# W1's blocks as the stationary operand, with 256 tokens moving, in a two-layer decoder trunk

## The chip, the cores and the metric

The kernel runs on one core of a Trainium2 chip. Its engines work side by side and meet only at semaphores: TensorE (PE, with its weight loads as PEld), VectorE (DVE), ScalarE (ACT), GpSimd (POOL), and SyncE (SP), which here issues most DMAs. The metric is the time of one execution on the device in microseconds; lower is better.

## The reference

Sequence 256, width 2048, two layers, everything in float32. Each layer has a mixer (layer 0 causal pooling, layer 1 retention) and then an MLP of hidden width 8192 with a squared ReLU. Before every sub-layer x is normalized, scaled and shifted.

```python
def sq_relu_mlp(h, w1, w2):
    a = jax.nn.relu(h @ w1)
    return (a * a) @ w2

for i in range(DEPTH):
    mod = jnp.einsum('bd,sdk->bsk', cond, ada_w[i]) + ada_b[i]
    ...
    h = modulate(rmsnorm(x, norm_g[i, 0]), shift_t, scale_t)
    ...                       # pool_mixer or retention
    x = x + gate_t[:, None, :] * y
    h = modulate(rmsnorm(x, norm_g[i, 1]), shift_m, scale_m)
    x = x + gate_m[:, None, :] * sq_relu_mlp(h, mlp_w1[i], mlp_w2[i])
return rmsnorm(x, final_g)
```

## The kernel before

**Matmuls in three products.** Every float32 operand is split into an upper part in the type fp32r and the rest, also in fp32r: `w_hi` and `w_lo` for weights, `h_hi` and `h_lo` for the normalized input (kept transposed: features on the partitions, 16 blocks of 128, by 256 tokens), `a_hi` and `a_lo` for the input of the second matmul. A product is low*high + high*low + high*high, added up in PSUM. On the tensor engine one operand is loaded as a block of 128x128 (the stationary one), the other is moved through it column by column.

**Chunks and units.** Weights come in chunks of 256 rows by 512 columns (512 KB are counted each) through a ring of four: SP loads `raw`, ACT writes `w_hi` (L970), DVE writes `w_lo` (L1343), PE uses both and reports with `w_used`. A chunk is 2 blocks of 128 rows x 2 tiles of 128 tokens x 3 products = 12 matmuls (L555): the tokens' block is stationary, and 512 columns of weights move. The result has tokens on the partitions and 512 outputs along the row, one PSUM bank for each of the two token tiles (`acc[pair][t]`). Eight chunks are a unit: 512 outputs over all of the 2048 inputs. A half unit has four.

**The MLP.** `mlp` goes through groups of eight units. Units 0 to 3 take W1 and make 4 x 512 hidden values, units 4 to 7 take W2 with them. ACT evacuates a W1 unit with ReLU into `ev[u % 2]` and squares it there. W2 needs the squares with the hidden index on the partitions, so in unit u + 1, behind chunk 2, PE transposes the squares (`transpose_squares`, L654): eight transposes of 128x128 in two banks `tb`; ACT copies each bank into `a_hi` (`evacuate_T`, L991), DVE makes `a_lo` from the bank and `a_hi` (`lower_T`, L1585). Seven W1 units are cut in two: their first halves (`p1`, PARTS) run ahead of everything, while the modulation weights are still loading, and are kept in `part_tile`; later `half_unit` does the rest and DVE adds the kept part (`add_part`, L1458). The first unit of layer 1's MLP has a form of its own, `first_unit`, since its input arrives tile by tile.

**Order.** Each engine has its own program, written out by hand from the same loops: `steps` on ACT and DVE puts one weight chunk's part at each step, four chunks ahead of PE, and `hooks` puts other work behind a step. Modulation weights (`ada_w`) are loaded and summed on DVE between chunks, as many as `ADA_SPREAD` and `ADA_EVEN` say. `Count` keeps for each engine how often each semaphore has counted at that place; `TB` counts banks of transposes or what takes their place, `TL` splits into `a_lo`.

## Time and profile before

| | |
|---|---|
| time, median of 3 runs | 2417.39 us (2416.83 to 2421.26) |
| the profiled execution | 2414.45 us |
| its span, first to last instruction | 2412.6 us |
| mean granted TensorE clock | 0.985 |
| busy: PE / PEld / DVE / ACT / POOL | 2339.1 / 1857.2 / 1580.9 / 1086.6 / 22.2 us |
| DMA | 620.38 MB, mean 257 GB/s |

The span is shorter than the execution's time by what lies around the first and last instruction. The busy time of PE is from the starts and the modelled ends of matmuls that overlap each other; the distance from one start to the next is what a matmul costs. Durations in the rows are of this one execution.

### The profile page before, as it was taken

The page shows a single profiled execution, that of the slowest core. Times are in us where ns is not written, and L with a number is a line of the kernel's source. Part 1 is how long each engine was busy: PE and PEld are TensorE (multiplying, and loading weights), DVE is VectorE, ACT ScalarE, POOL GpSimd, SP SyncE. Part 2 cuts the span into 40 slices and gives each one's busy share as a digit, 9 for nine tenths or more (in the row PEclk, how much of TensorE's full clock was granted, in tenths as well). Part 3 has the DMA queues.
Part 4 walks back from the last instruction along what each step waited for, and adds up shares of the span by engine and source line. Part 5 has one row for each costly group of instructions (what it writes and reads, how often), then busy time and mean ns, then how long its engine had stood idle before and what let it go on. Part 6 is the DMA issues. An engine that isn't in the chain of part 4 may idle for free.

```text
span 2412.6 us, 30003 instructions
## 1 busy us (share of the span) xinstructions
PE 2339.1 (97%) x10397; PEld 1857.2 (77%) x10397; DVE 1580.9 (66%) x1654; ACT 1086.6 (45%) x1352; POOL 22.2 (1%) x32
## 2 busy tenths in 40 slices
PE   6689999999999999999999999999999999999998
PEld 2147788887888887888888888887888888888886
DVE  4579886776776887656566657566876445445455
ACT  2324554443443545444444444445543443443443
POOL 0000000000000000000000000000000000000000
PEclk8799999999999999999999999999999999999999
DMA  9999988887887986776666766766987666656654
GB/s 391 405 408 391 343 312 310 296 291 253 296 291 258 327 309 213 239 224 222 220 222 228 240 221 216 228 221 198 331 292 229 185 191 193 185 190 192 188 182 154
DMA packets 269156, 620.38 MB, mean 257 GB/s; under 512 B 19064, under 2 KB 19400, under 8 KB 268112
## 3 DMA queue, kind: packets, MB, share of 16 engines
q1 hardware_dynamic: 267520, 612.44, 74.9%
q0 software_dynamic: 880, 5.77, 0.7%
q8 instruction: 90, 1.47, 0.2%
q14 instruction: 58, 0.48, 0.1%
q10 hardware_dynamic: 608, 0.22, 0.0%
HBM read 616.26 MB, written 2.10 MB: 256 GB/s over the span
## 4 chain that ended last, share of the span: by engine, by line
PE 89%; DMA 5%; DVE 4%; issue 1%; ACT 1%; SPq 0%; ACTq 0%; POOLq 0%; POOL 0%; DVEq 0%
PE acc L555 83%; DMA ada_early_h<-in_ada_w 3%; PE tb L654 2%; DMA raw<-in_mlp_w 1%; DVE ada_acc L1349 1%; DVE w_lo L1343 1%; PE mod_ps L690 0%; DMA ada_raw<-in_ada_w 0%; PE score_ps L904 0%; PE score_ps L690 0%; DVE h_lo L1537 0%; SPq L407 0%; ACT w_hi L970 0%; PE mod_ps L662 0%; PE acc L914 0%
## 5 line engine op out<-in xcount | busy, mean ns | idle before, releaser
L1343 DVE TENSOR_TENSOR w_lo<-raw,w_hi 128x1024 fp32r<-128x1024 f32 x776 | 947.1, 1224 | 725.4 <-ACT w_hi L970 725.0
L970 ACT ACTIVATE w_hi<-raw 128x1024 fp32r<-128x1024 f32 x776 | 821.7, 1060 | 1147.7 <-PE acc L555 1077.8
L555 PE MATMUL acc<-w_hi,h_lo 128*128 128x512 f32 x1792 | 706.9, 394 | 13.2 <-issue 7.0
L555 PE MATMUL acc<-w_hi,h_hi 128*128 128x512 f32 x1792 | 698.9, 390 | 0.0
L555 PE MATMUL acc<-w_lo,h_hi 128*128 128x512 f32 x1792 | 698.4, 390 | 0.0
L555 PE MATMUL acc<-w_hi,a_lo 128*128 128x512 f32 x1312 | 516.4, 394 | 0.0
L555 PE MATMUL acc<-w_hi,a_hi 128*128 128x512 f32 x1312 | 511.1, 390 | 0.0
L555 PE MATMUL acc<-w_lo,a_hi 128*128 128x512 f32 x1312 | 510.8, 389 | 0.0
L555 PEld LDWEIGHTS acc<-w_hi,h_lo 128*128 128x128 f32 x1792 | 337.2, 188 | 89.0 <-issue 12.3
L555 PEld LDWEIGHTS acc<-w_hi,h_hi 128*128 128x128 f32 x1792 | 337.0, 188 | 70.7
L555 PEld LDWEIGHTS acc<-w_lo,h_hi 128*128 128x128 f32 x1792 | 337.4, 188 | 69.5 <-issue 1.4
L1349 DVE SCALAR_TENSOR_TENSOR ada_acc<-ada_raw,cond,ada_acc 128x1024 f32<-128x1024 f32 x240 | 306.9, 1279 | 10.7 <-DMA ada_raw<-in_ada_w 10.4
L555 PEld LDWEIGHTS acc<-w_hi,a_lo 128*128 128x128 f32 x1312 | 246.5, 188 | 60.5 <-issue 8.5
L555 PEld LDWEIGHTS acc<-w_lo,a_hi 128*128 128x128 f32 x1312 | 246.6, 188 | 52.2 <-issue 1.9
L555 PEld LDWEIGHTS acc<-w_hi,a_hi 128*128 128x128 f32 x1312 | 246.4, 188 | 51.7
L986 ACT ACTIVATE ev<-acc 128x512 f32<-128x512 f32 x121 | 64.6, 584 | 7.7 <-PE acc L555 6.4
L1349 DVE SCALAR_TENSOR_TENSOR ada_acc<-ada_early_h,cond,ada_acc 128x1024 f32<-128x1024 f32 x37 | 47.5, 1283 | 26.1 <-DMA ada_early_h<-in_ada_w 25.6
L1585 DVE TENSOR_TENSOR a_lo<-tb,a_hi 128x512 fp32r<-128x512 f32 x80 | 51.3, 682 | 0.0
L690 PE MATMUL mod_ps<-ada_early_h,cond 128*32 128x512 f32 x88 | 29.3, 762 | 19.1 <-DMA ada_early_h<-in_ada_w 19.1
L991 ACT ACTIVATE a_hi<-tb 128x512 fp32r<-128x512 f32 x80 | 42.7, 586 | 0.0
L1001 ACT ACTIVATE sq_junk<-x 128x512 bf16<-128x512 f32 x46 | 28.4, 619 | 29.6 <-DVE x L1498 16.8
L1230 ACT ACTIVATE ev<-ev 128x512 f32<-128x512 f32 x64 | 36.7, 627 | 0.0
(164 smaller groups left out, 756.0 us busy)
## 6 DMA issues: line engine op xcount, KB each, us to landing
raw<-in_mlp_w SPq DMA_DIRECT2D x512, 512.0 KB, 4.5
ada_raw<-in_ada_w SPq DMA_DIRECT2D x280, 512.0 KB, 6.0
raw<-in_ret_w_in SPq DMA_DIRECT2D x192, 512.0 KB, 3.9
ada_early_h<-in_ada_w SPq DMA_DIRECT2D x84, 512.0 KB, 13.1
raw<-in_ret_w_out SPq DMA_DIRECT2D x64, 512.0 KB, 4.2
ada_early_a<-in_ada_w SPq DMA_DIRECT2D x20, 512.0 KB, 10.0
raw<-in_pool_w SPq DMA_DIRECT2D x8, 512.0 KB, 12.6
x<-in_x SPq DMA_DIRECT2D x2, 1024.0 KB, 9.8
```

Source lines behind the costliest of these rows:

```text
L555: mm = nc.tensor.matmul(acc[pair][t][:], l[:, CK * c + j, tok], w[:, c % RING, j, :], start=first and j == 0 and i == 0, stop=last and j = ...
L654: tr = nc.tensor.transpose(tb[b][:, j * S + t * P:j * S + (t + 1) * P], source(t)[:, m * P:(m + 1) * P], ident[:])
L690: mm = nc.tensor.matmul(bank[32 * b:32 * b + 32, :], cond[:, k:k + 1].to_broadcast([P, 32]), raw_rows[:, b % 2 * NB:(b % 2 + 1) * NB], sta ...
L970: nc.scalar.activation(w_hi[:, o % RING], raw[:, o % RING], ACT.Copy).then_inc(hi_ready, 1)
L986: nc.scalar.activation(target[:, t, :], acc[pair][t][:], func).then_inc(evac, 1)
L991: nc.scalar.activation(targets, tb[b][:].rearrange("p (k t) -> p k t", k=2), ACT.Copy).then_inc(tevac, 1)
L1001: nc.scalar.activation(sq_junk[:, t, :], x[:, t, block_ * NB:(block_ + 1) * NB], ACT.Square, accum_out=ssq[:, t, block_:block_ + 1]).then_ ...
L1230: nc.scalar.activation(ev[:, u % 2, t, :], ev[:, u % 2, t, :], ACT.Square).then_inc(sq_done, 1)
L1343: nc.vector.tensor_tensor(w_lo[:, o % RING], raw[:, o % RING], w_hi[:, o % RING].bitcast(F32), ALU.subtract).then_inc(lo_ready, 1)
L1349: nc.vector.scalar_tensor_tensor(out=part, in0=raw_rows, scalar=cond[:, k:k + 1], in1=part, op0=ALU.mult, op1=ALU.add).then_inc(ada_done, 1)
L1585: nc.vector.tensor_tensor(a_lo[:, k:k + 2, :], tb[b][:].rearrange("p (k t) -> p k t", k=2), a_hi[:, k:k + 2, :].bitcast(F32), ALU.subtract ...
```

## The change

In W1's units the roles are turned. `weights_chunk` loads a 128x128 block of W1 (`w_hi` or `w_lo`) and moves 256 tokens of `h`. A chunk is then 2 row blocks x 4 column blocks x 3 products = 24 matmuls of 256 columns. The result has the hidden index on the partitions and the tokens along the row, two column blocks to a bank; so the squares in `ev` are already laid out as W2 needs them. The transposes go; ACT copies the squares from `ev` to `a_hi` (`upper_squares`), DVE makes `a_lo` from `ev` (`lower_squares`). Since `ev` is now read until the split, ACT's evacuation and DVE's `add_part` wait for `tlo`. All W1 units are changed, the early halves too, but not layer 1's first one, whose squares are still transposed. A new count, `TD`, counts the banks that PE really fills. The retention, the pooling mixer and W2 are as before.

```diff
+            def weights_chunk(o, c, pair, first, last):
+                for j in range(CK):
+                    for m in range(4):
+                        out_ = acc[pair][m // 2][:, m % 2 * S:(m % 2 + 1) * S]
+                        cols = slice(m * P, (m + 1) * P)
+                        for i, (w, h) in enumerate(((w_hi, h_lo), (w_lo, h_hi), (w_hi, h_hi))):
+                            mm = nc.tensor.matmul(out_, w[:, o % RING, j, cols], h[:, CK * c + j, :],
+                                                  start=first and j == 0 and i == 0 and m % 2 == 0,
+                                                  stop=last and j == CK - 1 and i == 2 and m % 2 == 1)
+                mm.then_inc(w_used, 1)
+            def square_unit(pair, hooks, free):
+                for c in range(CH):
+                    pe.wait_ge(lo_ready, n.of("U") * HALF + (c + 1))
+                    ready_h(c)
+                    if c == 0:
+                        free()
+                    weights_chunk(c, c, pair, c == 0, c == CH - 1)
+                    for hook in hooks.get(c, []):
+                        hook()
+                n.unit("m1")
...
-                    chunk(c0 + o, h_hi, h_lo, pair, o == 0, o == HALF - 1)
+                    weights_chunk(o, c0 + o, pair, o == 0, o == HALF - 1)
...
-                            if 1 <= u <= 4:
-                                def transpose_squares(pair=(u - 1) % 2):
+                            if (layer, first, u) == (1, 0, 1):
+                                def transpose_squares():
                                     pe.wait_ge(sq_done, n.of("SQ") * TT)
-                                    transposes(lambda t: ev[:, pair, t, :], True)
+                                    transposes(lambda t: ev[:, 0, t, :], True)
                                 hooks[2] = [transpose_squares]
+                            elif 1 <= u <= 4:
+                                hooks[2] = [lambda: n.add(TB=2, TL=2)]
                             if (layer, first, u) == (1, 0, 0):
                                 first_unit("m1", 0, (h_hi, h_lo), mlp_free(0))
                             elif part_of(layer, first, u) is not None:
                                 half_unit("h1", u % 2, hooks, HALF, last_but_one if first == 0 else mlp_free(u))
                             elif u < 4:
-                                unit("m1", u % 2, hooks, (h_hi, h_lo), ready_h, mlp_free(u))
+                                square_unit(u % 2, hooks, mlp_free(u))
...
+            def upper_squares(pair, k, t):
+                act.wait_ge(sq_done, (n.of("SQ") - 1) * TT + t + 1)
+                nc.scalar.activation(a_hi[:, k:k + 2, :], ev[:, pair, t, :].rearrange("p (k t) -> p k t", k=2),
+                                     ACT.Copy).then_inc(tevac, 1)
...
-                                        evacuate_T(a_hi[:, k:k + 2, :], b)
+                                        if (layer, first, u) == (1, 0, 1):
+                                            evacuate_T(a_hi[:, k:k + 2, :], b)
+                                        else:
+                                            upper_squares((u - 1) % 2, k, b)
+                                    n.add(TL=2)
...
+                                    act.wait_ge(tlo, n.of("TL") - (2 if u else 0))
...
+                if i:
+                    dve.wait_ge(tlo, n.of("TL") - (2 if i % 2 else 0))
...
+            def lower_squares(pair, k, t):
+                dve.wait_ge(tevac, n.of("TB") + 1)
+                nc.vector.tensor_tensor(a_lo[:, k:k + 2, :], ev[:, pair, t, :].rearrange("p (k t) -> p k t", k=2),
+                                        a_hi[:, k:k + 2, :].bitcast(F32), ALU.subtract).then_inc(tlo, 1)
+                n.add(TB=1, TL=1)
...
-                                        lower_T(4 * (u - 1) + 2 * b, b)
+                                        if (layer, first, u) == (1, 0, 1):
+                                            lower_T(4 * (u - 1) + 2 * b, b)
+                                        else:
+                                            lower_squares((u - 1) % 2, 4 * (u - 1) + 2 * b, b)
```

PE's program, in the first group of layer 0, second unit, around its third chunk's end (acc10 and acc11 are the two banks of a pair; `h` and `w` are the parts named above, the moved operand's first after the change, second before). Before:

```order
L555 MATMUL acc11<-w_hi,h_lo 128x512
L555 MATMUL acc11<-w_lo,h_hi 128x512
L555 MATMUL acc11<-w_hi,h_hi 128x512
L654 MATMUL tb0<-ident,ev 128x128 x4
L654 MATMUL tb1<-ident,ev 128x128 x4
L555 MATMUL acc10<-w_hi,h_lo 128x512
L555 MATMUL acc10<-w_lo,h_hi 128x512
L555 MATMUL acc10<-w_hi,h_hi 128x512
```

After, at the same place:

```order
L571 MATMUL acc11<-h_lo,w_hi 128x256
L571 MATMUL acc11<-h_hi,w_lo 128x256
L571 MATMUL acc11<-h_hi,w_hi 128x256
L571 MATMUL acc10<-h_lo,w_hi 128x256
L571 MATMUL acc10<-h_hi,w_lo 128x256
L571 MATMUL acc10<-h_hi,w_hi 128x256
L571 MATMUL acc10<-h_lo,w_hi 128x256
L571 MATMUL acc10<-h_hi,w_lo 128x256
```

The eight transposes between two chunks are gone, and each row of 512 columns has become two of 256.

ACT's program in the same group: squares (L1230 before, L1270 after), three weight chunks, the copies to `a_hi`. Before:

```order
L1230 ACTIVATE ev<-ev 128x512 x2
L970 ACTIVATE w_hi<-raw 128x1024 x3
L991 ACTIVATE a_hi<-tb0 128x512
L991 ACTIVATE a_hi<-tb1 128x512
L970 ACTIVATE w_hi<-raw 128x1024
L1219 ACTIVATE ev<-ev 128x512 x2
```

After:

```order
L1270 ACTIVATE ev<-ev 128x512 x2
L998 ACTIVATE w_hi<-raw 128x1024 x3
L1025 ACTIVATE a_hi<-ev 128x512 x2
L998 ACTIVATE w_hi<-raw 128x1024
L1258 ACTIVATE ev<-ev 128x512 x2
```

The copies stand at the same place; they read `ev`, which ACT itself has written, where they read the banks `tb0` and `tb1` that PE had filled.

## Rows read from the trace of the kernel before

**Rows 1.** The page: busy time of each engine, and the chain that ended last
```profile
PE 2339.1 (97%) x10397; PEld 1857.2 (77%) x10397; DVE 1580.9 (66%) x1654; ACT 1086.6 (45%) x1352; POOL 22.2 (1%) x32
...
PE 89%; DMA 5%; DVE 4%; issue 1%; ACT 1%; SPq 0%; ACTq 0%; POOLq 0%; POOL 0%; DVEq 0%
PE acc L555 83%; DMA ada_early_h<-in_ada_w 3%; PE tb L654 2%; DMA raw<-in_mlp_w 1%; DVE ada_acc L1349 1%; DVE w_lo L1343 1%; PE mod_ps L690 0%; DMA ada_raw<-in_ada_w 0%; PE score_ps L904 0%; PE score_ps L690 0%; DVE h_lo L1537 0%; SPq L407 0%; ACT w_hi L970 0%; PE mod_ps L662 0%; PE acc L914 0%
```

**Rows 2.** Windows: stretch, length, busy us of each engine (instructions), granted clock, DMA
```profile
190.00:277.00 87.00, 82.38 (x351) 65.54 (x349) 79.58 (x78) 42.52 (x53) 0.00 (x0) 0.96 1.00 377
193.50:197.90 4.40, 4.40 (x12) 3.47 (x11) 4.33 (x7) 3.17 (x5) 0.00 (x0) 0.50 0.99 359
596.00:690.00 94.00, 94.00 (x428) 78.06 (x427) 68.00 (x62) 45.68 (x56) 0.00 (x0) 1.00 0.85 299
2055.00:2146.00 91.00, 91.00 (x417) 75.61 (x417) 43.34 (x39) 44.76 (x55) 0.00 (x0) 1.00 0.65 189
```

**Rows 3.** Waits: who waited for whom, us, times, longest
```profile
ACT w_hi L970 <- PE acc L555: 1077.8, 674, 11.1
...
DVE w_lo L1343 <- ACT w_hi L970: 725.0, 634, 3.3
```

**Rows 4.** Groups of instructions, main matmul, its load, transposes: busy us, mean ns
```profile
L555 PE MATMUL acc<-w_hi,h_lo 128*128 128x512 f32 x1792 | 706.9, 394 | 13.2 <-issue 7.0 <-DVE h_lo L1537 5.7 <-DVE w_lo L1343 0.5
...
L555 PEld LDWEIGHTS acc<-w_hi,h_lo 128*128 128x128 f32 x1792 | 337.2, 188 | 89.0 <-issue 12.3 <-DVE w_lo L1343 5.9 <-DVE h_lo L1537 3.3
...
L654 PE MATMUL tb<-ident,ev 128*128 128x128 f32 x256 | 33.1, 272 | 0.0
```

**Rows 5.** Timeline of PE, 2165 to 2205 us, first and last: start, length
```profile
2164.76 0.39 PE L555 MATMUL acc<-w_hi,a_lo 128*128 128x512 f32 x1
...
2204.88 0.39 PE L555 MATMUL acc<-w_hi,a_lo 128*128 128x512 f32 x1
```

**Rows 6.** Timeline of PE around one group of transposes
```profile
2277.63 0.40 PE L555 MATMUL acc<-w_hi,h_hi 128*128 128x512 f32 x1
2277.86 1.04 PE L654 MATMUL tb<-ident,ev 128*128 128x128 f32 x8
...
2278.97 0.39 PE L555 MATMUL acc<-w_lo,h_hi 128*128 128x512 f32 x1
...
2280.82 0.39 PE L555 MATMUL acc<-w_hi,h_lo 128*128 128x512 f32 x1
```

**Rows 7.** Line L786: count, length in ns (shortest, median, longest), first and last start
```profile
L786 PEld LDWEIGHTS tb<-diag,x x64: 186/192/338, 173.0 to 183.2; 128*128 128x128 f32 x64
L786 PE MATMUL tb<-diag,x x64: 274/275/582, 173.0 to 183.3; 128*128 128x128 f32 x64
```

**Rows 8.** Timeline of PE, line L786, 182.0 to 183.5 us
```profile
181.75 1.84 PE L786 MATMUL tb<-diag,x 128*128 128x128 f32 x15
```

**Rows 9.** Timeline of PE's weight loads (PEld), the same stretch
```profile
181.86 1.53 PEld L786 LDWEIGHTS tb<-diag,x 128*128 128x128 f32 x13
```

**Rows 10.** Timeline of PE at the lower clock
```profile
193.74 0.63 PE L555 MATMUL acc<-w_hi,h_hi 128*128 128x512 f32 x1
...
195.87 0.63 PE L555 MATMUL acc<-w_lo,h_hi 128*128 128x512 f32 x1
```

**Rows 11.** Timeline of PE, full-precision matmuls of 256 and 128 columns
```profile
47.55 0.60 PE L711 MATMUL tb<-scratch,x 128*128 128x256 f32 x2
47.98 0.38 PE L713 MATMUL tb<-scratch,x 128*128 128x128 f32 x2
```

**Rows 12.** Groups of instructions: passes over 512 columns on ACT and DVE
```profile
L1585 DVE TENSOR_TENSOR a_lo<-tb,a_hi 128x512 fp32r<-128x512 f32 x80 | 51.3, 682 | 0.0
...
L991 ACT ACTIVATE a_hi<-tb 128x512 fp32r<-128x512 f32 x80 | 42.7, 586 | 0.0
L1230 ACT ACTIVATE ev<-ev 128x512 f32<-128x512 f32 x64 | 36.7, 627 | 0.0
...
L1576 DVE TENSOR_TENSOR ev<-ev,gate 128x512 f32<-128x512 f32 x22 | 14.2, 684 | 6.6 <-ACT gate L1082 5.7 <-ACT ev L986 0.9
```

More of the change, by code:

```diff
@@ L60 @@
     NAMES = ("U", "E", "SQ", "XA", "RO", "TB", "TL", "SC", "Y", "AD", "AP", "SG", "RM",
-             "TR", "CS", "GB", "YA", "NO", "GN", "HT", "SB", "MS", "XS", "T0", "PS")
+             "TR", "CS", "GB", "YA", "NO", "GN", "HT", "SB", "MS", "XS", "T0", "PS", "TD")
     def __init__(self):
@@ L110 @@
 M_ROUND = dict(U=16, E=4, SQ=4, YA=4, TB=8, TL=8)
-R_ROUND = dict(U=32, E=20, XA=4, RO=4, TB=16, TL=8, SC=4, Y=4, AD=SEG, SG=1, RM=1, TR=1, CS=1, SB=3)
+R_ROUND = dict(U=32, E=20, XA=4, RO=4, TB=16, TL=8, TD=16, SC=4, Y=4, AD=SEG, SG=1, RM=1, TR=1, CS=1, SB=3)
 def mlp_round(what):
@@ L989, in evacuate_T @@
             def evacuate_T(targets, b):
-                act.wait_ge(tr_done, n.of("TB") + 1)
+                act.wait_ge(tr_done, n.of("TD") + 1)
                 nc.scalar.activation(targets, tb[b][:].rearrange("p (k t) -> p k t", k=2), ACT.Copy).then_inc(tevac, 1)
+                n.add(TB=1, TD=1)
+            def upper_squares(pair, k, t):
+                act.wait_ge(sq_done, (n.of("SQ") - 1) * TT + t + 1)
+                nc.scalar.activation(a_hi[:, k:k + 2, :], ev[:, pair, t, :].rearrange("p (k t) -> p k t", k=2),
+                                     ACT.Copy).then_inc(tevac, 1)
                 n.add(TB=1)
@@ L1009, in transposed_x @@
             def transposed_x(f):
-                act.wait_ge(tr_done, n.of("TB") + 1)
+                act.wait_ge(tr_done, n.of("TD") + 1)
                 k = 2 * f % (KT // 2)
@@ L1014, in transposed_x @@
                                      ACT.Copy).then_inc(tevac, 1)
-                n.add(TB=1)
+                n.add(TB=1, TD=1)
             def norm_bank(f):
@@ L1131, in _ @@
                 first_norm(f)
-            n.add(TB=CH)
+            n.add(TB=CH, TD=CH)
             copy_rows(mod_ps, 2, PE_BEFORE[SEG])
@@ L1586, in lower_T @@
                                         a_hi[:, k:k + 2, :].bitcast(F32), ALU.subtract).then_inc(tlo, 1)
-                n.add(TB=1)
+                n.add(TB=1, TL=1)
[3 more added lines that the diff above has]
+                                        a_hi[:, k:k + 2, :].bitcast(F32), ALU.subtract).then_inc(tlo, 1)
+                n.add(TB=1, TL=1)
             def mean_square():
```

## The prediction

> **What bounds the kernel now.** I read the page first. PE is busy 97% of the span, and of the chain that ended last 89% is PE, 83% the one line L555 [rows 1]. A busy PE is not yet a bound, so I looked at stretches of W1 units [rows 2]: in 596 to 690 us and in 2055 to 2146 us PE never stops, at the full granted clock, while DVE is busy 68 of 94 us and 43 of 91, and DMA 0.85 and 0.65 of its time. Only 190 to 277 us, where the first halves of W1's products are made, is different: DMA share 1.00 at 377 GB/s, PE 82.4 of 87 us. In the table of waits the weight pipeline stands behind PE: ACT waits 1077.8 us for chunks to be used, DVE 725.0 us for ACT [rows 3]. So what the change does to PE's time goes nearly whole into the span, and what it does on ACT and DVE does not.
>
> PE's busy time overlaps itself (a record of 0.389 us each [rows 4]), so the price of a matmul is its distance to the next. In the run of rows 5, 178 matmuls start from 2164.76 to 2204.88 us: 40.12 / 177 = 0.2267 us each, for 512 columns moved against a loaded 128x128 block. Each has its own weight load of 0.188 us [rows 4], and none of that shows.
>
> **The change, part by part.** W1 is 2 layers x 16 blocks x 8 chunks = 256 chunks of 12 matmuls; layer 1's first unit keeps the old form, so 248 chunks change.
>
> (1) Removed: 248 x 12 = 2976 matmuls of 512 columns, 2976 x 0.2267 = 674.6 us.
>
> (2) Added: 248 x 24 = 5952 matmuls of 256 columns, each with a full 128x128 load. The columns moved in all stay the same; the loads double. The sum hangs on the distance c of two such pairs, and the trace has no fp32r matmul of 256 columns. Bounds:
> - From below, 0.1118: the full-precision matmuls L786. They too load 128x128 every time, with a record of 0.192 us [rows 7], and move 128 columns at two cycles each (106.7 ns), which is the array time of 256 columns at one. Fifteen stand in 1.84 us with the last one 0.275 long, (1.84 - 0.275) / 14 = 0.1118; their thirteen loads (1.53 - 0.192) / 12 = 0.1115 [rows 8, 9]. So loads can follow each other at 0.112 although each lasts 0.19, and the doubled loads are no bound above that.
> - From above, 0.120. At the full clock, 2.4 GHz, 512 columns at one a cycle are 213.3 ns, and 226.7 are measured: 13.3 ns extra. At half the clock (1.2 GHz, the window 193.5 to 197.9 [rows 2]) five distances take 195.87 - 193.74 = 2.13 us [rows 10], 0.426 each, which is 512 / 1.2: nothing extra. So the extra is not array cycles; something at another pace, probably the supply of the moved fp32 values, shows only at 2.4 GHz. Is it per column or per matmul? Per column, 256 cost half: 0.1133. Per matmul, 106.7 + 13.3 = 120.0 ns.
> The full-precision ones, which take their values at half the rate, show almost no fixed part: two matmuls of 256 columns go in 47.98 - 47.55 = 0.43 us [rows 11], 0.215 each where 256 columns in two cycles are 0.2133. That speaks a little for the per-column reading. I take 0.1145: half the measured distance, 0.1133, plus 0.001 for loads that now sit at their own limit of 0.112. 5952 x 0.1145 = 681.5 us, 6.9 more than (1). At the ends: 5952 x 0.1118 = 665.4, 9.2 less; 5952 x 0.120 = 714.2, 39.6 more.
>
> Here a rule of the Trainium skill can be weighed. By the row, 512 columns cost 0.2267 [rows 5]. "TensorE: Matmul & The Clock Gate", section Back-to-back issue gap, gives N/2.4 + 2.5 ns, 215.8 for 512, which this trace does not confirm (11 ns too little), and says that in a stream of loads and matmuls both set the spacing, so that few columns cost more than the formula. By the formula c would be 0.1092; it is treated with the third rival.
>
> (3) Removed: 31 groups of eight transposes of squares (248). In rows 6 one is seen with what surrounds it: without it the tenth matmul after 2277.63 would start at 2277.63 + 10 x 0.2267 = 2279.90; it starts at 2280.82. So one group costs 0.92 us: eight transposes (1.04 - 0.27) / 7 = 0.110 apart, 0.88, and some 0.04 until the matmuls are back at their pace (the eight distances from 2278.97 on take 0.231 each). 31 x 0.92 = 28.5 us, all on PE, all on the path. The group of layer 1's first unit stays.
>
> (4) ACT and DVE do the same number of operations, reading squares in SBUF, not the PSUM banks. By the rows an ACT copy from PSUM is 586 ns, a pass from SBUF to SBUF 627 [rows 12]: 62 x 0.04 = 2.5 us, hidden in ACT's 1077.8 us of waiting for PE [rows 3]. DVE's subtraction stays (682 against 684 ns [rows 12]). If the cover went, it would be these 2.5 us.
>
> (5) Waits. ACT no longer waits for PE's transposes at that step, PE no longer for the squares or the bank. New is that ACT's evacuation, and DVE's adding of the saved half, wait for the split of the squares that were in that buffer before. That split stands at step 2 of the unit after those squares, and the new wait at the end of the unit behind that one (21.8 us a unit, 10.9 a half one), so it has long been done. Behind ACT's waiting instruction would queue the weight chunks' upper parts, and PE behind those; I cost it at nothing, since about a unit of slack hides it. SP's and POOL's orders do not change, and no DMA is added.
>
> (6) PE's semaphore and register instructions per chunk stay as many, with the same time between chunks.
>
> **Sum.** +6.9 - 28.5 = -21.6 us. The profiled execution took 2414.45 us (span 2412.6), which becomes 2392.8; from the median of the runs, 2417.39, it is 2395.8, say 2396. PE is the later one in nearly every stage after, too: the fed chunks come 0.9 us sooner per unit of 22 us, 4%, and DMA and DVE have 15% and more to spare there. Only the 28 chunks of 190 to 277 us have no such room. The change breaks even at c = (674.6 + 28.5) / 5952 = 0.1181.
>
> **Rivals.**
> First, the one on the other side: the 13.3 ns are paid per matmul (a start of the moved stream), not per column. Then c = 0.120, +39.6 - 28.5 = +11.1 us: 2428.5, slower. It decides from c = 0.1181. For it: the extra vanishes at half clock, as a fixed start-up that can hide would; after a group of transposes the distances are 0.231 for a while before they are 0.2267 again [rows 6], which looks like loads and matmuls getting into step, not like a plain rate. Against it: the full-precision ones show next to no fixed part. If the 28 chunks beside the full DMA hide their share, it is 28 x 24 x 0.0067 = 4.5 us less, 2424.
> Second: loads of fp32r blocks cannot follow each other as those of L786 do, and the pair takes its load's 0.188 us [rows 4]. 5952 x 0.188 - 674.6 - 28.5 = +416 us: 2833. For it: a load begins only when the matmul before it has begun, and its record is longer than c. Against it: L786, with the same 0.19 us records 0.112 apart [rows 7 to 9]. Partial forms (0.13) give 2417.4 + 773.8 - 703.1 = 2488.
> Third: everything hides, and the pair goes at the 0.110 of the transposes, which load a block each too [rows 6]. 5952 x 0.110 = 654.7, -19.9 - 28.5 = -48.4 us: 2369. For it nothing but that row; against it, that the 512 ones do not reach their array time, and L786's 0.112. The skill's formula named above gives 2364 by c = 0.1092; the trace agrees neither with its 512 value nor, in rows 8 and 9, with so short a distance for full loads.
> Fourth: PE gets faster, but what feeds it does not follow in the stages with modulation loads (DMA 0.85 busy [rows 2]), and half of the gain is given back to waits for chunks: 2407, still faster.
>
> **How the numbers follow.** Forecast (c from 0.1125 to 0.118) 0.56; first rival 0.26; second 0.10; third 0.04; fourth 0.04. What a measurement of this kernel can tell from no change is about 0.2%, 4.8 us, that is c between 0.1173 and 0.1189; 0.03 of the forecast and 0.02 of the fourth lie there. Faster 0.53 + 0.04 + 0.02 = 0.59, within 0.05, slower 0.36. The forecast's own range is 2384 (c = 0.1125) to 2416. The whole range goes up over the first rival, 2428, to c = 0.1215, 2437, and down to 2383; what is left out is the second rival, the third and a little of either end.
>
> **What would show it.** In the profile after, the new line's matmuls should start 0.113 to 0.116 apart within a chunk, a chunk should take about 2.75 us (24 x 0.1145) where it took 2.72, and a unit of eight some 0.7 us less than before, counting the group of transposes that is gone. Matmuls of W2 and of the retention stay at 0.2267. PEld's busy share should rise to nearly the whole span in W1 units without meaning anything. ACT's copies of the squares should be 0.63 us and find no wait. What would make the prediction wrong is above all a distance of 0.120 (per matmul), next a distance that follows the load's record; an idle time of PE before the new line, released by w_lo or raw, would be the fourth.

## The result: 8.6 us slower

The changed kernel takes 2425.89 us (median of ten runs, 2422.4 to 2427.5) where the one before takes 2417.29 us (ten runs, 2414.85 to 2421.26). The ratio is 1.0034, with a 95% interval of 1.0026 to 1.0042: slower by 8.6 us, where 2396 had been forecast. The first rival had said 2428.5. The profiled execution is the longest of the ten, 2427.5 us with a span of 2425.7; that of before is one of the shortest, 2414.45 with 2412.6.

The page after, engines' busy time and the chain of waits:

```profile
PE 2353.2 (97%) x13125; PEld 1991.2 (82%) x13125; DVE 1580.2 (65%) x1654; ACT 1090.4 (45%) x1352; POOL 22.2 (1%) x32
...
PE 90%; DMA 5%; DVE 3%; issue 1%; ACT 1%; SPq 0%; POOL 0%; ACTq 0%; POOLq 0%; DVEq 0%
PE acc L555 57%; PE acc L571 30%; DMA ada_early_h<-in_ada_w 2%; DMA ada_raw<-in_ada_w 2%; DVE ada_acc L1389 1%; PE tb L680 1%; DVE w_lo L1383 1%; PE score_ps L932 0%; DMA raw<-in_ret_w_in 0%; DVE h_lo L1579 0%; PE score_ps L716 0%; DMA rcount<-in_rcount 0%; PE acc L942 0%; PE acc L943 0%; PE acc L944 0%
```

Against [rows 1] nothing has changed its role. PE has 2728 matmuls more (2976 of W1 and 248 transposes fewer) and is still busy 97% of the span and 90% of the chain; L555's 83% are now split between L555 (57%) and the new line L571 (30%). DVE and ACT moved by 0.7 and 3.8 us. So the added time has to be PE's.

Windows of the profile after, the same stretches as in [rows 2] and three more (length, busy us of PE, PEld, DVE, ACT and POOL with their instructions, granted clock, DMA share, GB/s):

```profile
190.00:277.00 87.00, 84.53 (x683) 82.38 (x682) 78.97 (x76) 40.77 (x49) 0.00 (x0) 0.98 1.01 375
192.40:195.60 3.20, 2.83 (x13) 2.87 (x14) 3.13 (x6) 3.20 (x6) 0.00 (x0) 0.50 1.03 403
281.10:284.30 3.20, 3.20 (x17) 3.20 (x16) 1.61 (x3) 1.46 (x3) 0.00 (x0) 0.50 0.53 136
596.00:690.00 94.00, 93.08 (x765) 92.27 (x764) 64.36 (x59) 43.42 (x51) 0.00 (x0) 1.00 0.84 288
974.00:977.00 3.00, 3.00 (x9) 2.35 (x8) 3.00 (x3) 0.00 (x0) 0.00 (x0) 0.50 0.96 268
2055.00:2146.00 91.00, 90.83 (x746) 90.02 (x745) 43.02 (x40) 42.73 (x50) 0.00 (x0) 1.00 0.63 181
```

In the W1 units at 596 and 2055 us PE hardly rests (the 0.92 us missing at 596 are one gap between two rounds of units), at the full clock, and DMA (0.84 and 0.63) and DVE (64 and 43 us) have the room that they had. PEld is busy 92.27 of 94 and 90.02 of 91 us. That alone says nothing of a bound, since the records of loads overlap: those of [rows 9] last 0.192 us and are 0.112 apart.

What PE does with that time is in its timeline, first and last matmul of one stretch (start, length):

```profile
620.73 0.28 PE L571 MATMUL acc<-h_lo,w_hi 128*128 128x256 f32 x1
...
629.85 0.28 PE L571 MATMUL acc<-h_hi,w_lo 128*128 128x256 f32 x1
```

These are 77 matmuls, 76 distances: 9.12 / 76 = 0.1200 us. It is the same everywhere: of the 5940 distances between two L571 matmuls that follow each other, 5857 are exactly 120 ns. That is the bound taken from above, to the nanosecond. One of 512 columns keeps its 0.2267.

The groups of the new line and of the split of the squares on DVE and ACT (busy us, mean ns of one):

```profile
L571 PE MATMUL acc<-h_lo,w_hi 128*128 128x256 f32 x1984 | 563.6, 284 | 5.4 <-issue 5.4
L571 PEld LDWEIGHTS acc<-h_lo,w_hi 128*128 128x128 f32 x1984 | 382.2, 193 | 8.5 <-issue 8.3
L1634 DVE TENSOR_TENSOR a_lo<-ev,a_hi 128x512 fp32r<-128x512 f32 x62 | 39.9, 685 | 0.0
L1025 ACT ACTIVATE a_hi<-ev 128x512 fp32r<-128x512 f32 x62 | 35.3, 617 | 0.0
```
The waits (us, times, longest):

```profile
ACT w_hi L998 <- PE acc L555: 771.0, 483, 11.9
ACT w_hi L998 <- PE acc L571: 307.8, 189, 3.0
```

ACT's copy of squares out of SBUF takes 617 ns (0.63 forecast, 586 before [rows 12]), the subtraction 685 ns, neither had to wait, and ACT still waits 771.0 + 307.8 = 1078.8 us for PE, as in [rows 3]. Line L571's own idle time is 5.4 us of "issue", against 7.0 for L555's first product in [rows 4].

### The profile page after: what moved, and what is told of

The parts are those of the page before. It is cut to its first block, busy times and chain, and to the rows that moved or that the text cites. A ratio compares the mean times of both kernels' runs of the same rounds, so it can differ in the third digit from the quotient of the medians.

```text
span 2425.7 us, 35380 instructions
## 1 busy us (share of the span) xinstructions
PE 2353.2 (97%) x13125; PEld 1991.2 (82%) x13125; DVE 1580.2 (65%) x1654; ACT 1090.4 (45%) x1352; POOL 22.2 (1%) x32
## 4 chain that ended last, share of the span: by engine, by line
PE 90%; DMA 5%; DVE 3%; issue 1%; ACT 1%; SPq 0%; POOL 0%; ACTq 0%; POOLq 0%; DVEq 0%
PE acc L555 57%; PE acc L571 30%; DMA ada_early_h<-in_ada_w 2%; DMA ada_raw<-in_ada_w 2%; DVE ada_acc L1389 1%; PE tb L680 1%; DVE w_lo L1383 1%; PE score_ps L932 0%; DMA raw<-in_ret_w_in 0%; DVE h_lo L1579 0%; PE score_ps L716 0%; DMA rcount<-in_rcount 0%; PE acc L942 0%; PE acc L943 0%; PE acc L944 0%
## 5 line engine op out<-in xcount | busy, mean ns | idle before, releaser
L998 ACT ACTIVATE w_hi<-raw 128x1024 fp32r<-128x1024 f32 x776 | 822.5, 1061 | 1157.1 <-PE acc L555 771.0
L571 PE MATMUL acc<-h_lo,w_hi 128*128 128x256 f32 x1984 | 563.6, 284 | 5.4 <-issue 5.4
L571 PE MATMUL acc<-h_hi,w_lo 128*128 128x256 f32 x1984 | 562.7, 284 | 0.0
L571 PE MATMUL acc<-h_hi,w_hi 128*128 128x256 f32 x1984 | 562.6, 284 | 0.0
L555 PE MATMUL acc<-w_hi,a_lo 128*128 128x512 f32 x1312 | 515.7, 393 | 0.0
L555 PE MATMUL acc<-w_hi,a_hi 128*128 128x512 f32 x1312 | 510.9, 389 | 0.0
L555 PE MATMUL acc<-w_lo,a_hi 128*128 128x512 f32 x1312 | 510.8, 389 | 0.0
L571 PEld LDWEIGHTS acc<-h_lo,w_hi 128*128 128x128 f32 x1984 | 382.2, 193 | 8.5 <-issue 8.3
L571 PEld LDWEIGHTS acc<-h_hi,w_lo 128*128 128x128 f32 x1984 | 382.3, 193 | 0.2
L571 PEld LDWEIGHTS acc<-h_hi,w_hi 128*128 128x128 f32 x1984 | 382.1, 193 | 0.0
L555 PE MATMUL acc<-w_hi,h_lo 128*128 128x512 f32 x800 | 317.2, 396 | 9.3 <-DVE h_lo L1579 5.7
L555 PE MATMUL acc<-w_hi,h_hi 128*128 128x512 f32 x800 | 312.3, 390 | 0.0
L555 PE MATMUL acc<-w_lo,h_hi 128*128 128x512 f32 x800 | 312.1, 390 | 0.0
L555 PEld LDWEIGHTS acc<-w_hi,a_lo 128*128 128x128 f32 x1312 | 246.5, 188 | 59.5 <-issue 7.8
L555 PEld LDWEIGHTS acc<-w_lo,a_hi 128*128 128x128 f32 x1312 | 246.5, 188 | 52.2 <-issue 1.9
L555 PEld LDWEIGHTS acc<-w_hi,a_hi 128*128 128x128 f32 x1312 | 246.4, 188 | 52.0
L555 PEld LDWEIGHTS acc<-w_hi,h_lo 128*128 128x128 f32 x800 | 150.5, 188 | 44.4 <-DVE w_lo L1383 6.3
L555 PEld LDWEIGHTS acc<-w_lo,h_hi 128*128 128x128 f32 x800 | 150.6, 188 | 31.5 <-issue 1.4
L555 PEld LDWEIGHTS acc<-w_hi,h_hi 128*128 128x128 f32 x800 | 150.6, 188 | 31.5
```

What stands on the lines that cost most here:

```text
L555: mm = nc.tensor.matmul(acc[pair][t][:], l[:, CK * c + j, tok], w[:, c % RING, j, :], start=first and j == 0 and i == 0, stop=last and j = ...
L571: mm = nc.tensor.matmul(out_, w[:, o % RING, j, cols], h[:, CK * c + j, :], start=first and j == 0 and i == 0 and m % 2 == 0, stop=last an ...
L998: nc.scalar.activation(w_hi[:, o % RING], raw[:, o % RING], ACT.Copy).then_inc(hi_ready, 1)
```

## The experiments

The theories. **A**: each matmul of these values pays some 13.3 ns beyond its columns over 2.4 GHz, whatever their number (the first rival); everything else of the sum is right. **B**: the spacing is half of the old one, and the time was lost elsewhere: to roles (weights loaded, tokens moved), to banks, to feeding. **C**: the removal of the transposes gave less than 28.5 us.

### The transposes alone

The exchange of the squares' layout is left out, with W1's products made as before:

```diff
@@ square_unit
-                    weights_chunk(c, c, pair, c == 0, c == CH - 1)
+                    chunk(c, h_hi, h_lo, pair, c == 0, c == CH - 1)
@@ half_unit
-                    weights_chunk(o, c0 + o, pair, o == 0, o == HALF - 1)
+                    chunk(c0 + o, h_hi, h_lo, pair, o == 0, o == HALF - 1)
```

> One part alone: W1's matmuls keep their old form (token block stationary, 512 columns of W1 moving, 12 to a chunk), and only the 31 groups of transposes go; ACT and DVE take the squares from ev as in the change. The squares then reach W2 with tokens and hidden index exchanged, so that part of the computation is left out. Both theories (the extra 13.3 ns is paid per matmul; or per column, with loads at their limit of 0.120) expect the same: 31 x 0.92 = 28.5 us less than before, 2417.3 - 28.5 = 2389. If the transposes were hidden or the ending of their waits were worth more, it would lie away from that by over 5 us.

Measured: 2387.72 us (2386.15 to 2388.06, 4 runs) against 2416.86 (15 runs), ratio 0.9877 (0.9861 to 0.9892), 29.1 us less. Span 2384.3 against 2412.6, 28.3 less. So the 31 groups were worth 0.91 to 0.94 us each, all of it on the path, and C is out. From this kernel to the changed one it is then 2425.9 - 2387.7 = 38.2 us, and the only difference between their programs is 5952 narrow matmuls in place of 2976 wide ones.

### The columns alone

The kernel before, its roles, banks and transposes kept; only each W1 matmul of the changed units is cut in two of 256 columns:

```diff
+                        for part in range(2):
+                            cols = slice(part * S, (part + 1) * S)
+                            for i, (l, w) in enumerate(((lhs_lo, w_hi), (lhs_hi, w_lo), (lhs_hi, w_hi))):
+                                mm = nc.tensor.matmul(acc[pair][t][:, cols], l[:, CK * c + j, tok],
+                                                      w[:, c % RING, j, cols],
```

> The other part alone, without the change of roles: the kernel before, with each of W1's matmuls in the changed units cut into two of 256 columns (token block stationary, W1 moving, transposes kept). Per matmul or per load: 5952 pairs at 0.120 in place of 2976 at 0.2267, +39.6 us, 2417.3 + 39.6 = 2457. If the 0.120 belonged to the roles (W1's blocks as the stationary operand, read from the ring that ACT and DVE write), the pairs here would go at 0.113 and the time would stay at 2417.

Measured: 2451.7 us (2450.28 to 2452.56, 4 runs), ratio 1.0142 (1.0126 to 1.0158), 34.8 us more than before. Its timeline of PE, first and last of one stretch, and around one group of transposes:

```profile
639.51 0.28 PE L571 MATMUL acc<-w_hi,h_lo 128*128 128x256 f32 x1
...
647.91 0.28 PE L571 MATMUL acc<-w_lo,h_hi 128*128 128x256 f32 x1
```
```profile
2312.08 0.28 PE L571 MATMUL acc<-w_hi,h_hi 128*128 128x256 f32 x1
2312.20 1.04 PE L669 MATMUL tb<-ident,ev 128*128 128x128 f32 x8
2312.99 0.36 PE L571 MATMUL acc<-w_hi,h_lo 128*128 128x256 f32 x1
2313.19 0.28 PE L571 MATMUL acc<-w_lo,h_hi 128*128 128x256 f32 x1
```

From 639.51 to 647.91 us there are 70 distances of 0.1200. Nothing but the width has changed, so neither the roles nor the source of the values matter: B is out. Of the expected 39.6 us 35.8 show in the span. Some of the missing 3.8 is in the second fence. Behind the last matmul before a group (2312.08) the second one after it starts 1.11 us later; with nothing between it would be 0.24, so a group costs 0.87 here and not 0.92, 1.5 us in 31. Of the other 2.3 us the traces show some 1.4: the stretch of lower clock at 193 us lasts 3.4 us and not 6.8, some 0.8 less; PE's pause of 0.81 us before 265.8, in which it waits for a modulation sum (`ada_acc`), and its wait of 0.54 us for `w_lo` before 966.5 are absent; and two pauses of "issue" are longer, 0.85 for 0.60 and 0.73 for 0.20. The rest stays open; the interval of the ratio is 8 us wide. The two parts alone add up to 34.8 - 29.1 = 5.7 us, which agrees with the 8.6 of the whole change within these intervals.

### The price of a width by itself

Is it per matmul at every width, and is it the type? Trains of 48 to 64 matmuls that follow each other and wait for nothing, each with a load of its own; none of the kernel's computation is in it:

```python
def run(tile, count, cols, load=P, st=xr, mv=wr):
    for i in range(count):
        k = i % 8
        mm = nc.tensor.matmul(ps[tile][0:load, 0:cols], st[:, k * P:k * P + load],
                              mv[:, (i % 3) * 512:(i % 3) * 512 + cols],
                              start=i == 0, stop=i == count - 1)
```

> None of the computation, only distances between matmuls: trains of 48 to 64 on one engine with nothing beside them, in fp32r, bfloat16 and float32, of several widths and several widths of the loaded block. Theory 1, a fixed 13.3 ns for each fp32r matmul: 448, 384, 320, 256 columns at 0.2000, 0.1733, 0.1467, 0.1200. Theory 2, a rate of 0.4427 ns per column with loads that need 0.120: 0.1983, 0.1700, 0.1417, 0.1200, and 0.1133 for 256 columns against a block of 64 or 32 columns, where theory 1 keeps 0.1200. Theory 3, the extra comes with the load and goes with its size: 512 columns against 64 or 32 loaded columns at about 0.220 and 0.217. bfloat16, if the extra belongs to fp32r: 512 at 0.215, 256 at 0.109 to 0.112. float32 256 at 0.215 twice.

The timeline of PE, the inner part of eleven trains (start, and length from the first start to the last end; right of the arrow first the moved operand, then the stationary one; wr and xr are fp32r, wb and xb bf16, w and x float32 at full precision, two records a matmul; `128*64` is a loaded block of 64 columns):

```profile
34.72 9.00 PE L64 MATMUL r<-wr,xr 128*128 128x512 f32 x39
55.24 6.75 PE L64 MATMUL r<-wr,xr 128*128 128x384 f32 x38
63.83 5.44 PE L64 MATMUL r<-wr,xr 128*128 128x320 f32 x36
70.75 5.92 PE L64 MATMUL r<-wr,xr 128*128 128x256 f32 x48
77.73 4.52 PE L64 MATMUL r<-wr,xr 128*128 128x128 f32 x39
83.70 9.60 PE L64 MATMUL load<-wr,xr 128*64 128x512 f32 x41
105.80 9.23 PE L64 MATMUL r<-wb,xb 128*128 128x512 bf16 x42
115.73 5.95 PE L64 MATMUL r<-wb,xb 128*128 128x256 bf16 x53
122.50 19.90 PE L64 MATMUL r<-w,x 128*128 128x512 f32 x46
142.67 10.52 PE L64 MATMUL r<-w,x 128*128 128x256 f32 x48
164.33 6.40 PE L64 MATMUL load<-wr,xr 128*64 128x256 f32 x55
```

A row of n matmuls is n - 1 distances and the last one's length, which the groups give (389 ns for 512 fp32r columns, 334, 309, 283 and 274 for 384, 320, 256 and 128; 392 and 276 for 512 and 256 with a load of 64; 379 and 273 for bf16; 592 and 379 at full precision). Columns over 2.4 GHz are called the array's time:

| values, columns, loaded | distance, us | array | more |
|---|---|---|---|
| fp32r, 512, 128 | (9.00 - 0.389) / 38 = 0.2266 | 0.2133 | 13.3 ns |
| fp32r, 384, 128 | (6.75 - 0.334) / 37 = 0.1734 | 0.1600 | 13.4 |
| fp32r, 320, 128 | (5.44 - 0.309) / 35 = 0.1466 | 0.1333 | 13.3 |
| fp32r, 256, 128 | (5.92 - 0.283) / 47 = 0.1199 | 0.1067 | 13.3 |
| fp32r, 128, 128 | (4.52 - 0.274) / 38 = 0.1117 | 0.0533 | (a floor) |
| fp32r, 512, 64 | (9.60 - 0.392) / 40 = 0.2302 | 0.2133 | 16.9 |
| fp32r, 256, 64 | (6.40 - 0.276) / 54 = 0.1134 | 0.1067 | 6.7 |
| bf16, 512, 128 | (9.23 - 0.379) / 41 = 0.2159 | 0.2133 | 2.5 |
| bf16, 256, 128 | (5.95 - 0.273) / 52 = 0.1092 | 0.1067 | 2.5 |
| full, 512 at two cycles | (19.90 - 0.592) / 45 = 0.4291 | 0.4267 | 2.4 |
| full, 256 at two cycles | (10.52 - 0.379) / 47 = 0.2158 | 0.2133 | 2.4 |

This settles the size for the kernel's own form. Against a full block of 128 loaded columns, an fp32r matmul pays 13.3 ns at 256, 320 and 384 columns as at 512; bf16 and full precision pay 2.5. The full-precision rows that I took for a witness against a fixed part [rows 11] pay another one. With 128 columns the distance stops at a floor of 0.1117, the same as in [rows 8, 9]; bf16 goes under it, at 0.1092.

It does not settle the reason, and none of the three theories comes out whole. Theory 2, a rate per column, is refuted by 384 and 320 columns (0.1700 and 0.1417 expected, 0.1734 and 0.1466 measured). But theory 1, a fixed amount, expected 0.1200 for 256 columns against a block of 64 or 32, and there the trains show what theory 2 said: 0.1134, and 0.1133 with 32 loaded. Theory 1 also misses 448 columns, (9.08 - 0.365) / 43 = 0.2027 for 0.2000. Theory 3, less extra with a smaller load, fails at 512 columns, where it grows: 16.9 ns with 64 loaded, and (10.36 - 0.392) / 43 = 0.2318, 18.5 ns, with 32. So at 256 columns half of the 13.3 ns goes when the loaded block is halved: they belong to the load and the moved columns together and are no plain price of a start.

The 2.5 ns are what the Trainium skill's "TensorE: Matmul & The Clock Gate", section Back-to-back issue gap, states as N/2.4 + 2.5; the trace agrees for bf16 and, per record and with two cycles a column, for full precision, and not for fp32r.

### Keeping 512 columns where the operand allows it

If each matmul pays the same extra, W1's three products of a block can be had with two matmuls in place of three: the upper part of a W1 block is loaded once and moves both parts of the tokens side by side, 512 columns, then the lower part moves the upper tokens, 256. The two halves of a bank are summed by DVE (96 passes of some 0.68 us, in time that it has to spare), and ACT reads the sum in place of the bank. The 24 full units (192 chunks) are made so, the 56 chunks of the half units stay as changed:

```diff
+                for j in range(CK):
+                    for m in range(4):
+                        bank = wide[pair][m]
+                        cols = slice(m * P, (m + 1) * P)
+                        nc.tensor.matmul(bank[:], w_hi[:, o % RING, j, cols],
+                                         h_both[:, CK * c + j, :, :].rearrange("p o t -> p (o t)"),
+                                         start=first and j == 0, stop=False)
+                        mm = nc.tensor.matmul(bank[:, S:2 * S], w_lo[:, o % RING, j, cols], h_hi[:, CK * c + j, :],
+                                              start=False, stop=last and j == CK - 1)
...
+                        nc.vector.tensor_reduce(ev[:, u % 2, t, i * S:(i + 1) * S],
+                                                bank[:].rearrange("p (o t) -> p t o", o=2), AX_X,
```

> A version that should keep the gain and lose most of the price, if it is per matmul: in the 24 full W1 units but layer 1's first, each block of w_hi is loaded once and moves h_lo and h_hi side by side, 512 columns into one bank, and w_lo moves h_hi, 256 columns; DVE adds the two halves of each bank (four reductions of 512 a unit). Per block 0.2267 + 0.120 = 0.3467 in place of 3 x 0.120 = 0.360: 192 chunks x 8 x 0.0133 = 20.4 us less than the changed kernel, 2425.9 - 20.4 = 2405.5, 12 us under the kernel before. If the price were per column (theory 2), two pairs cost 0.2267 + 0.120 as well, so this run tells nothing between them; if DVE's added 2.6 us a unit came on the path, it would be up to 24 x 2.6 = 62 us more.

Measured: 2412.44 us (2409.78 to 2413.95, 11 runs), ratio 0.9979 (0.997 to 0.9988): 4.4 us faster than before and 13.5 faster than the change, but not the 11.4 expected. Two stretches of its timeline, first rows of chunks (eight pairs), in the unit at 642 us and in the last one at 2288 us:

```profile
647.93 0.40 PE L584 MATMUL acc<-h_both,w_hi 128*128 128x512 f32 x1
...
650.70 0.40 PE L584 MATMUL acc<-h_both,w_hi 128*128 128x512 f32 x1
...
2288.90 0.40 PE L584 MATMUL acc<-h_both,w_hi 128*128 128x512 f32 x1
...
2291.73 0.40 PE L584 MATMUL acc<-h_both,w_hi 128*128 128x512 f32 x1
```

The first is 2.77 us, 0.3467 a pair, as forecast (0.2267 + 0.1200). The second is 2.83, 0.353. A whole round of units keeps to one of the two. Of the 24 units 13 go at 2.827 us a chunk and 11 at 2.773 (one of these only from its fourth chunk on, behind an interruption of 0.8 us). The sum with them: 104 x (2.827 - 2.720) + 88 x (2.773 - 2.720) + 56 x 0.16 - 28.5 = -3.7 us; the span is 5.0 less. So two widths in turn have two paces, and more than half of the units fell into the slower one. The trace also shows what comes before each. The stream of alternating widths is entered eight times. Three times PE is held up right behind the first wide matmul (the next starts 0.33 us after it at 597.57 and 2044.79, and 0.31 us at 1717.80), and these are the three fast stretches:

```profile
597.57 0.49 PE L584 MATMUL acc<-h_both,w_hi 128*128 128x512 f32 x1 [0.64 <-issue]
597.89 0.28 PE L587 MATMUL acc<-h_both,w_lo 128*128 128x256 f32 x1
```

The five times without such a hold (0.23 us from the first to the second, at 417.54, 809.73, 1708.53, 1866.72 and 2220.72) the pace is the slow one. That is eight of eight, in one execution; by what it works is not shown.

### Mixed widths by themselves

Trains again, with other widths, and with 512 and 256 columns in turn, one, four or eight of each; nothing of the kernel's computation:

```python
def mixed(tile, rounds, wide, narrow):
    for r in range(rounds):
        for i in range(wide):
            nc.tensor.matmul(ps[tile][:], xr[:, i % 8 * P:i % 8 * P + P], wr[:, 0:512],
                             start=r == 0 and i == 0, stop=False)
        for i in range(narrow):
            nc.tensor.matmul(ps[tile][:, 256:512], xr[:, i % 8 * P:i % 8 * P + P], wr[:, 512:768],
                             start=False, stop=r == rounds - 1 and i == narrow - 1)
```

> None of the computation, only distances: more widths, two more sizes of the loaded block, and trains in which 512 and 256 columns alternate (1+1, 4+4, 8+8, 1+2). The earlier trains gave columns / 2.4 GHz + 13.3 ns for 256, 320, 384 and 512 columns against 128 loaded, 16.0 for 448, 0.1117 for 128, and other values for 64 and 32 loaded. If the 13.3 ns are a fixed amount that any loaded block of 128 brings: 480 at 0.2133, 352 at 0.1600, 288 at 0.1333, and 224 and 192 at the larger of their sum and 0.1117 (0.1117 both). If loads and matmuls have to get into step (theory of the step), widths off a multiple of 64 settle at other extras, as 448 did. Alternating: by fixed amounts 0.2267 + 0.1200 = 0.3467 a pair, 1.387 for 4+4, 2.773 for 8+8; by the theory of the step 1+1 costs about 0.3505, as in the kernel with the wide upper part (0.2341 + 0.1165), and the longer trains come nearer to the sum.

Its timeline of PE: one of each in turn, first and last pair; then a round of eight:

```profile
102.61 0.39 PE L72 MATMUL r<-wr,xr 128*128 128x512 f32 x1
...
110.72 0.40 PE L72 MATMUL r<-wr,xr 128*128 128x512 f32 x1
...
125.09 2.00 PE L72 MATMUL r<-wr,xr 128*128 128x512 f32 x8
126.93 1.11 PE L75 MATMUL r<-wr,xr 128*128 128x256 f32 x8
127.89 2.00 PE L72 MATMUL r<-wr,xr 128*128 128x512 f32 x8
```

A pair in turn takes (110.72 - 102.61) / 23 = 0.3526, the slower of the two paces. A round of four takes 1.40 (from 112.47 to 113.87), 0.350 a pair, and one of eight 2.80, 0.350; 1.387 and 2.773 would be the sums of the separate prices. One wide and two narrow ones in turn take (149.82 - 139.06) / 23 = 0.468 us, hardly more than their sum of 0.4667, so a change of width does not always cost something. In a round of eight the wide ones take (126.93 - 125.09) / 8 = 0.230 each and the narrow ones 0.120: a wide one needs some starts at its own width until it is down to 0.2267. Grouping costs a steady 0.35 a pair, between the two paces of the alternating stream. The new widths, inner parts of trains with 480, 352 and 288 columns:

```profile
35.70 7.53 PE L64 MATMUL r<-wr,xr 128*128 128x480 f32 x34
45.23 6.44 PE L64 MATMUL r<-wr,xr 128*128 128x352 f32 x39
53.11 5.17 PE L64 MATMUL r<-wr,xr 128*128 128x288 f32 x38
```

With their last records of 378, 323 and 294 ns these are (7.53 - 0.378) / 33 = 0.2167, (6.44 - 0.323) / 38 = 0.1610 and (5.17 - 0.294) / 37 = 0.1318: 16.7, 14.3 and 11.8 ns over the array's 0.2000, 0.1467 and 0.1200. So the extra isn't the same at every width, but it doesn't grow with the columns: 288 and 320 differ by 1.5 ns, 480 and 512 by 3.4 the other way. The trains of 224 and 192 columns stop at the floor, at 0.1116 and 0.1115 us. A block of 96 loaded columns stands between 64 and 128:

```profile
86.81 4.45 PE L64 MATMUL load<-wr,xr 128*96 128x256 f32 x37
```

With 256 columns moved it takes (4.45 - 0.278) / 36 = 0.1159, 9.2 ns more than the array, between 6.7 and 13.3. At 384 columns the loaded block changes nothing: (6.58 - 0.337) / 36 = 0.1734 with 64 loaded, as with 128.

### Grouped by width

The same kernel with each chunk's eight wide matmuls first and then its eight narrow ones, so that no unit can fall into the slow pace:

```diff
                 for j in range(CK):
                     for m in range(4):
-                        bank = wide[pair][m]
...
+                for j in range(CK):
+                    for m in range(4):
+                        mm = nc.tensor.matmul(wide[pair][m][:, S:2 * S], w_lo[:, o % RING, j, m * P:(m + 1) * P],
```

> The version with the wide upper part, with the order inside a chunk changed: first its eight matmuls of 512 columns, then its eight of 256, not in turns. Theory of the step: each change of width costs some ns, and there are 2 a chunk in place of 16; the pair goes from 0.3505 back towards 0.3467, 1536 x 0.0038 = 5.8 us less, 2412.4 - 5.8 = 2407. If the excess belonged to accumulating in a bank that has just been written, or to the wide operand, it would stay at 2412.

Measured: 2408.1 us (2407.2 to 2409.37, 5 runs), ratio 0.996 (0.9947 to 0.9974) to the kernel before. Its timeline of PE, from the start of one chunk to that of the second after it:

```profile
649.74 0.63 PE L582 MATMUL acc<-h_both,w_hi 128*128 128x512 f32 x2
...
651.58 0.40 PE L587 MATMUL acc<-h_both,w_lo 128*128 128x256 f32 x2
...
655.33 0.63 PE L582 MATMUL acc<-h_both,w_hi 128*128 128x512 f32 x2
```

Two chunks take 655.33 - 649.74 = 5.59 us, 2.79 each, and it is so in every unit. The expected time was 2407; the pair came to 0.349 and not to the 0.3467 from which that was worked out. The sum 192 x (2.793 - 2.720) + 56 x 0.16 - 28.5 = -5.5; the span is 6.7 less and the median 9.1. Against the version with alternating widths the sum is 1.8 us less and the span 1.7, while the medians are 4.3 apart; that version's profiled execution was its fastest of 11, and how many units of the others went at the slow pace isn't known. At 0.4% under the kernel before, this is the lowest median of all kernels that compute the reference; the version of the next section can't be told from it.

### The half units back

The 56 chunks of half units still pay 0.16 us each. They are put back to the old form, with the seven groups of transposes that this needs again:

```diff
+def by_tokens(layer, first, u):
+    return (layer, first, u) == (1, 0, 0) or part_of(layer, first, u) is not None
...
-                    weights_chunk(o, c0 + o, pair, o == 0, o == HALF - 1)
+                    chunk(c0 + o, h_hi, h_lo, pair, o == 0, o == HALF - 1)
```

> The same, and the seven units that are cut into halves (early halves too) back in the form of before, with their squares transposed. By the price of 0.16 us a chunk and 0.92 us a group: 56 x 0.16 = 9.0 us less for the matmuls, 7 x 0.92 = 6.4 us more for transposes, -2.5 us against e6. If the early halves hide their price behind the full DMA (28 x 0.16 = 4.5 us), it would be 1.9 us more than e6.

Measured: 2409.06 us (2408.37 to 2413.6, 6 runs), ratio 0.9969 (0.9957 to 0.9981), 1.0 more than the version above and inside its interval: no difference that can be told, where 2.5 less was expected (or 1.9 more, if the early halves hid their price). The trace shows one thing that takes back a part: PE waits 1.67 us for a modulation sum (`ada_acc`) before 265.8 us, a wait that the version above doesn't have. The time itself is inconclusive.

## Why the prediction was wrong, by its steps

(1) and (6), the removed 674.6 us and the time between chunks, were right: 0.2267, and no new gaps between chunks of W1. (The record of 0.389 us that the prediction reads from [rows 4] is 0.394 there; nothing hangs on it.)

(2) is the step that failed, and with it the sign: c, the distance of two matmuls of 256 columns, was taken as 0.1145 and is 0.1200, so that the term is +39.6 us and not +6.9. The prediction made c of 0.1133 for the moved columns, by the reading that the extra is paid per column, and 0.001 for the loads. The trains refute that reading at 320 and 384 columns. At 256 columns they show 0.1134 against a block of 64, and 6.6 ns more against the full block, where 1 ns had been put for the loads. Why these 6.6 ns are paid stays open. The time broke even at 0.1181. The bounds were right and held the truth at the upper one. What led away from it was the witness of [rows 11]: full-precision matmuls pay 2.5 ns, fp32r ones 13.3, at 256 columns as at 512 with full blocks. A pace read from one type says nothing of another. The better witness was my own: at half the clock the extra vanishes. It had been read as "not array cycles", and then given to the columns, for which no row spoke.

(3) was right: 28.5 forecast, 29.1 and in the span 28.3 measured with the exchange left out.

(4) and (5) were right. The copies took 617 ns and hid, and no wait appeared at the new places.

The first rival named the distance and the sign: c = 0.120 and +39.6 - 28.5 = +11.1, or +10.5 by the measured removal. The runs show +8.6, with an interval of 6.3 to 10.2, so both sums are a little too high. Its reason, a price of each start of the moved stream, is not shown: alone it would have kept 0.120 with a smaller block loaded. The variant by which the 28 early chunks hide their whole share beside the full DMA did not come. The timeline of PE at the first matmul of the third and of the 25th of them, before (first two rows) and after, and at a pause of before:

```profile
201.01 0.39 PE L555 MATMUL acc<-w_hi,h_lo 128*128 128x512 f32 x1
...
262.06 0.39 PE L555 MATMUL acc<-w_hi,h_lo 128*128 128x512 f32 x1
...
199.88 0.28 PE L571 MATMUL acc<-h_lo,w_hi 128*128 128x256 f32 x1
...
264.41 0.28 PE L571 MATMUL acc<-h_lo,w_hi 128*128 128x256 f32 x1
...
265.75 1.05 PE L662 MATMUL mod_ps<-ada_acc,ones 128*32 128x512 f32 x4 [0.81 <-DVE ada_acc L1349]
```

The 22 chunks from the one to the other take 264.41 - 199.88 = 64.53 us in place of 262.06 - 201.01 = 61.05, 3.48 more, where 22 x 0.16 is 3.52. But a small part is given back behind them: before, PE waits 0.81 us for a modulation sum, and after, it comes later and doesn't wait. PE was busy 84.53 us of the 87 beside the full DMA (82.38 before [rows 2]); it had little room. The span of the profiled execution grew by 13.1. Of what lies beyond the sum, 1.24 us are a longer wait of PE for `w_lo` in the retention (1.78 us before 972.9, where before had 0.54; it differs from run to run, 0.73 with the transposes alone removed and 0.26 with the widths grouped). Another part is the clock: three stretches of some 3.4 us at 0.50 (at 192, 281 and 974 us) where before had one of 6.8 around the window in [rows 2]; the later two follow gaps of 1.8 us in PE's work. Such a gap alone doesn't decide it: before has one of 1.93 us at 277.6 and no lower clock behind it. The timeline of PE after, at the first such gap and at the lower clock behind it:

```profile
279.49 0.36 PE L571 MATMUL acc<-h_lo,w_hi 128*128 128x256 f32 x1 [1.81 <-issue]
...
283.53 0.41 PE L571 MATMUL acc<-h_lo,w_hi 128*128 128x256 f32 x1
283.74 0.41 PE L571 MATMUL acc<-h_hi,w_lo 128*128 128x256 f32 x1
```

At 0.50, which is 1.2 GHz, the 256-column matmuls are 0.21 apart (256 / 1.2 = 213 ns, again nothing extra), so 3.4 us hold 16 of them where 28 would go; the extra stretch cost about 16 x 0.093 = 1.5 us, in this one execution. The second rival (0.188) and the third (0.110) are excluded by the distance, and the fourth by DMA and DVE, which kept their room.

## What to carry to other kernels

In these runs an fp32r matmul with a full block loaded and 256 or more columns moved costs its columns / 2.4 GHz and some 13 ns (11.8 to 16.7 over the widths tried, 13.3 at 256 and 512). So a change that halves 512 columns for the same products pays 13.3 ns per matmul added, here 2976 times, and needs to save more than that elsewhere. Before such a change is argued from another type's or another width's pace, a train of the very form (type, columns, loaded block) is the cheap measurement; and where two streams share a stationary block, moving them side by side at the full width, with matmuls of one width kept together, was worth 17.8 us here over the changed kernel (2408.1 against 2425.9).

## What the runs showed of the hardware

- What an fp32r matmul pays over its array time depends on the loaded block and the moved columns together. With 256 moved it is 13.3 ns for 128 loaded, 9.2 for 96 and 6.7 for 64 or 32; with 384 moved 13.3 for 128 and for 64; with 512 moved 13.3 for 128, 16.9 for 64 and 18.5 for 32.
- Against full blocks widths are not all alike: 13.3 ns at 512, 384, 320 and 256 columns, but 16.7 at 480, 16.0 at 448, 14.3 at 352 and 11.8 at 288. What sets it stays open.
- Two widths in turn have two stable paces, 2.773 and 2.827 us for eight pairs, kept over whole rounds of units. In the one trace the fast pace came each time (three of three) behind a hold after the first matmul, the slow one (five of five) without it.
- The weight load's record (192 ns at 0.120 apart) and PEld's 99% say by themselves nothing of a bound: with the same full loads the distance goes down to 0.1117. Still the load has a share in the 0.1200, as the smaller blocks show.
